# Rotary partners in a decoder layer: a TensorE matmul in place of partition-moving DMAs

## The reference, cut to what matters

```python
def rope_partial(t, cos, sin):            # t: (B, S, heads, 2, 64); only the first 16 of 64 dims turn
    half = ROT_DIM // 2                   # 8
    t1 = t[..., :half]
    t2 = t[..., half:ROT_DIM]
    rot = jnp.concatenate([t1 * c - t2 * s, t2 * c + t1 * s], axis=-1)
    return jnp.concatenate([rot, t[..., ROT_DIM:]], axis=-1)

# per head, two softmaxes over 64-dim halves, causal, in blocks of 128 queries:
p = softmax(mask(q_c k_c^T / 8));   a = p[0] - lam * p[1];   out = a @ v
```

## Time and profile before

| | |
|---|---|
| median of three executions | 1784.95 us |
| the profiled execution, its own time | 1784.95 us |
| its span, first to last instruction | 1783.2 us |
| PE busy | 1574.5 us (88%) |
| DVE busy | 1300.6 us (73%) |
| ACT busy | 546.8 us (31%) |
| POOL busy | 707.3 us (40%) |

### The profile page before, as it was taken

How to read it: one execution, slowest core, us unless ns; L and a number is a source line. 1 busy time by engine, 2 the same in 40 slices (tenths; PEclk the granted TensorE clock), 3 DMA queues, 4 the chain that set the end, 5 groups by cost and what they waited for, 6 DMA issues and landing times.

```text
span 1783.2 us, 20596 instructions
## 1 busy us (share of the span) xinstructions
PE 1574.5 (88%) x7020; PEld 1165.1 (65%) x7020; DVE 1300.6 (73%) x2421; ACT 546.8 (31%) x1337; POOL 707.3 (40%) x598
## 2 busy tenths in 40 slices
PE   3998999988997999999997999997999989999800
PEld 2787877776876999888886888885444434444300
DVE  5766456677455598999997789898566656666798
ACT  2442245534623642111113888884000000000001
POOL 1000111100001565633566566566644445444672
PEclk7999999999998999999998999999999999999955
DMA  8424421234421544999999999999999999999994
GB/s 325 164 95 151 159 74 57 78 109 163 169 95 48 179 157 181 408 367 357 367 383 363 327 363 369 339 358 334 387 409 409 409 412 409 409 409 409 409 401 188
DMA packets 126280, 499.18 MB, mean 280 GB/s; under 512 B 15456, under 2 KB 15840, under 8 KB 115808
## 3 DMA queue, kind: packets, MB, share of 16 engines
q0 software_dynamic: 75776, 269.52, 39.2%
q1 hardware_dynamic: 50400, 228.35, 33.6%
HBM read 492.04 MB, written 4.72 MB: 279 GB/s over the span
## 4 chain that ended last, share of the span: by engine, by line
DVE 34%; DMA 25%; PE 23%; ACT 6%; issue 4%; POOL 3%; DVEq 3%; ACTq 1%; SPq 0%
DMA ring<-in_up,idx 20%; DVE ring L1453 7%; DVE accum L1662 6%; PE bank L746 5%; PE bank L494 5%; PE bank L495 5%; PE bank L496 5%; DMA ring<-in_down,idx 4%; POOL ring L1687 3%; PE bank L733 2%; DVE acc_ada L1111 2%; DMA raw<-in_ada 1%; ACT whi L781 1%; DVE top_i L1490 1%; DVE top_i L1475 1%
## 5 line engine op out<-in xcount | busy, mean ns | idle before, releaser
L759 PE MATMUL bank<-stream,wmat 128*128 128x512 f32 x1024 | 443.7, 596 | 13.7 <-DMA stream<-in_up 7.0
L746 PE MATMUL bank<-h2T,stream 128*128 128x256 f32 x2048 | 451.6, 380 | 0.0
L1662 DVE SCALAR_TENSOR_TENSOR accum<-ring,share,accum 128x1024 f32<-128x1024 f32 x256 | 328.9, 1285 | 165.1 <-DMA ring<-in_up,idx 159.4
L1687 POOL DMA_INDIRECT ring<-in_down,idx x256 | 330.1, 1290 | 237.9 <-DVE pre L1453 184.5
L746 PEld LDWEIGHTS bank<-h2T,stream 128*128 128x128 f32 x2048 | 385.6, 190 | 50.6 <-issue 0.3
L759 PEld LDWEIGHTS bank<-stream,wmat 128*128 128x128 f32 x1024 | 195.9, 192 | 260.9 <-issue 246.2
L1687 POOL DMA_INDIRECT ring<-in_up,idx x256 | 263.8, 1030 | 233.1 <-DVE accum L1662 193.2
L1453 DVE CUSTOM_DVE_ANT_0 ring<-ring,h2row 128x1024 f32<-128x1024 f32 x256 | 306.0, 1220 | 42.0 <-DMA ring<-in_down,idx 38.6
L494 PE MATMUL bank<-hT_hi,whi 128*128 128x512 f32 (+1 forms) x640 | 232.1, 363 | 22.1 <-DVE hT_lo L1164 11.8
L495 PE MATMUL bank<-hT_lo,whi 128*128 128x512 f32 (+1 forms) x640 | 225.5, 352 | 0.0
L496 PE MATMUL bank<-hT_hi,wlo 128*128 128x512 f32 (+1 forms) x640 | 225.4, 352 | 0.0
(11 more groups left out here) (212 smaller groups left out, 1668.2 us busy)
## 6 DMA issues: line engine op xcount, KB each, us to landing
stream<-in_downT SPq DMA_DIRECT2D x128, 512.0 KB, 6.7
stream<-in_up SPq DMA_DIRECT2D x128, 512.0 KB, 6.8
raw<-in_ada SPq DMA_DIRECT2D x24, 1024.0 KB, 5.6
raw<-in_w_query SPq DMA_DIRECT2D x16, 1024.0 KB, 4.9
raw<-in_w_xp SPq DMA_DIRECT2D x4, 1024.0 KB, 6.0
raw<-in_w_gateA SPq DMA_DIRECT2D x4, 1024.0 KB, 4.8
raw<-in_w_branchP SPq DMA_DIRECT2D x4, 1024.0 KB, 4.8
raw<-in_w_q SPq DMA_DIRECT2D x4, 1024.0 KB, 4.7
```

Of the source, the lines that this page charges most:

```text
L746: last = pe.matmul(bank[:, 4 + i % 2, 0:DT], stream[:, i % RING, k * P:(k + 1) * P], h2T[:, k, GB * P:S], start=(k == 0), stop=(k == KT - 1))
L759: last = pe.matmul(bank[:, 2 * tb + half, :], wmat[:, i, tb * P:(tb + 1) * P], stream[:, (ET + i) % RING, half * S:(half + 1) * S], start= ...
L1662: dve.scalar_tensor_tensor(accum[:, b, :], ring[slot][:, :], share[:, b, k:k + 1], accum[:, b, :], ALU.mult, ALU.add).then_inc(sum_done, 1)
L1687: pool.indirect_dma_start(out=ring[slot][:, :], out_offset=None, in_=table, in_offset=bass.IndirectOffsetOnAxis(ap=idx[:, b, k:k + 1], axi ...
```

## The change

The partner exchange is done by PE. A constant 128x128 matrix `rotm` (128 more columns in the constants' transfer) holds -1 and +1 at the partners' places, and `rotate(n)` multiplies it with the `q_raw` tile into PSUM bank 6, the bank of the transposes. DVE reads the bank in place of `q_rot`. The sign moves out of the sine table into the matrix. The buffer `q_rot`, its zeroing and the 64 DMAs go. PE gets waits: a rotation waits for ACT's copy into `q_raw`, for the copy of all transposes issued so far and for the rope before; a `turn` waits until the ropes of all earlier slots have read the bank. The first rope of each group moves from slot 5 to slot 4.

```diff
-TURN_AT = {12 * (c - 1) + s: 4 * c + r for c in range(4) for r, s in enumerate((5, 7, 10, 13))}
+TURN_AT = {12 * (c - 1) + s: 4 * c + r for c in range(4) for r, s in enumerate((4, 7, 10, 13))}
...
+            def rotate(n):
+                c, r = n // 4, n % 4
+                wait_emptied(pe, "q" if r < 2 else "k", 2 * c + r % 2)
+                pe.wait_ge(trs_ready, sum(1 for g in UNIT_AT if g + TR_AFTER <= [s for s in TURN_AT if TURN_AT[s] == n][0]))
+                if n:
+                    pe.wait_ge(rot_used, n)
+                pe.matmul(bank[:, 6, :], rotm, q_raw[:, n % 2, :], start=True, stop=True)\
+                  .then_inc(rot_ready, 1)
...
             def turn(u):
...
+                pe.wait_ge(rot_used, sum(1 for s in TURN_AT if s < [g for g in UNIT_AT if UNIT_AT[g] == u][0] + TR_AFTER))
...
             def woven(g):          # PE; behind scores, turn and values of the slot
+                if g in TURN_AT:
+                    rotate(TURN_AT[g])
...
             def rope(n):           # DVE
-                dve.wait_ge(rot_in[n % 2], 64 * (n // 2 + 1))
+                dve.wait_ge(rot_ready, n + 1)
...
-                dve.tensor_tensor(q_tmp[:, 1, :], q_rot[:, n % 2, :], rope_sin[:, :], ALU.mult)
+                dve.tensor_tensor(q_tmp[:, 1, :], bank[:, 6, :], rope_sin[:, :], ALU.mult)
...
-            for n in range(16):    # POOL: partners(n) and its four DMAs each
-                partners(n)
...
                     # constants
+        if r < ROT // 2:
+            c[p + ROT // 2, C_ROT + p] = -1.0
+        elif r < ROT:
+            c[p - ROT // 2, C_ROT + p] = 1.0
-            c[p, C_FREQ] = inv[r % (ROT // 2)] * (-1.0 if r < ROT // 2 else 1.0)
+            c[p, C_FREQ] = inv[r % (ROT // 2)]
```

More of the change, by code:

```diff
@@ L49 @@
 PI_BELOW = 3.1415925
-C_ID, C_MASK, C_FREQ, C_INV, C_IOTA = 0, 128, 256, 257, 273
-C_W = 273 + 128
+C_ID, C_ROT, C_MASK, C_FREQ, C_INV, C_IOTA = 0, 128, 256, 384, 385, 401
+C_W = 401 + 128
 K_C, K_BADA, K_BGATE, K_PSCALE, K_GMIX, K_GFFN, K_SUBLN = 0, 8, 56, 72, 80, 88, 96
@@ L242, in layer @@
         ident = cst[:, C_ID:C_ID + P]
+        rotm = cst[:, C_ROT:C_ROT + P]
         mask = cst[:, C_MASK:C_MASK + P]
@@ L271, in layer @@
         q_tmp = place("q_tmp", [P, 2, S], f32, 144)
-        q_rot = place("q_rot", [P, 2, S], f32, 160)
         sigB = place("sigB", [P, KT, S], f32, 148)
@@ L367, in layer @@
         lam_exp = sem("lam_exp")
-        rot_in = [sem(f"rot_in{n}") for n in range(2)]
+        rot_ready = sem("rot_ready")
         rot_used = sem("rot_used")
@@ L859, in woven_tile @@
                 if stage == "gateB":
-                    if i == 6:
-                        act.wait_ge(rot_used, 16)
                     act.activation(sigB[:, i, :], tile(stage, i), ACT.Identity,
@@ L1702, in wlo_make @@
                 pool.sem_inc(qraw_free, 1)
[L1704 to L1717, removed]
-            for n in range(16):
-                partners(n)
-            for n in POOL_CHUNKS[1:]:
+            for n in POOL_CHUNKS:
                 wlo_make(n)
```

## The result

The changed kernel takes 1801.01 us (median of seven executions, 1798.86 to 1804.76); the kernel before, run beside it, takes 1784.34 us (seven, 1776.91 to 1787.41). The ratio is 1.0094, with a 95% interval from 1.0079 to 1.011: slower by 16.7 us. The profiled execution took 1803.89 us, its span is 1801.9 us. The forecast was 1800.5 us.

The account below looks back on a forecast made before the run. PE was taken as nearly full, busy 131.3 of 135.0 us, with DVE almost as late. Slot costs 2.6 + 0 + 9.0 + 2.5 + 0.5 + 1.0 = 15.6 us on 1784.95 gave 1800.5 us, range 1791 to near 1810.

Parts of the forecast that it names:

- The DMAs were hidden: Woven stage: only one of 16 ropes waited for partner DMAs, 5.9 us, so removing the 64 gives nothing by itself.
- A rotation costs 0.86 us of PE: Each of sixteen rotations holds PE 0.86 us, 13.8 us in all; its result is readable 1.02 us after its start.
- the case 1791 us: Rival: rotations overlap with projections, about 4 us of PE instead of 13.8, leaving 6 us slower; chance 0.05.
- DVE reads PSUM at no cost: Rope's sine multiply reading PSUM instead of SBUF: 0 us extra.
- Slots -8 to 1: First four rotations: 2.6 us in slots -8, -5, -2; 0 in slot 1, at most 1.0, given a 1.60 us wait.
- Slots 4, 16, 28: Moved ropes ahead of maxima: rotation 0.86 plus a new turn wait of 0.75, 1.6 us per slot.
- Slots 7, 10, 13 and 37: Slot 7 pays the plain rotation, 0.9 us; the others delay rope, maxima and the turn by 1.0 us each.
- Slot 34: Late rope makes the turn wait for its end, 1.9 us, less 1.43 us of PE idle time: 0.5 us.
- the clock as a rival: Form of the bank rival, 371 to 441 us: longer PE waits lower the clock, up to 3.5 us more; shared chance 0.14.
- Absorbing waits: Rival: PE's waits absorb rotations, +1.0 us, and three moved ropes give back 6.2 us: 1779.8 us; chance 0.10.
- A shared bank that decides in most slots: Rival: turns wait for rope ends in twelve other slots, up to 1 us each, 12 us more: 1812 us; chance 0.14.
- Freed POOL and DMAs: Rival: freeing POOL, DMA engines and the first rope's wait gains 5.9 us: 1779 us; chance 0.03.

Follow-up runs that it names:

- the doubled rotation: The changed kernel with each rotation issued twice into the same bank: 1812.71 us, ratio 1.0168 to the kernel before.
- constants alone: The kernel before with only the constants' transfer widened by 128 unused columns: 1782.25 us, ratio 0.9999.
- some maxima ahead: The changed kernel with DVE doing maxima ahead of the rope in slots 1 or 4 modulo 12: 1796.64 us, ratio 1.0073 to the kernel before.
- the move alone: The kernel before, DMAs kept, with the first rope of each group in slot 4 instead of 5: 1785.95 us, ratio 1.0020.
- the matmuls alone: The kernel before, DMAs and ropes kept, plus an unread f32 matmul of the rotation's size in each of sixteen rope slots: 1794.30 us, ratio 1.0064.
- first slot 5: The changed kernel with the first rope of each group back in slot 5: 1802.84 us, ratio 1.0113 to the kernel before.
- the version that beats both: The kernel before with maxima ahead of ropes, second conditioning chunk two slots later, its column sums one weight chunk later: 1775.39 us, ratio 0.9958.

## Why the prediction was right, step by step

**The DMAs were hidden: right.** The 64 transfers and POOL's work are gone (40.8 us of busy POOL), and no time came of it.

**A rotation costs 0.86 us of PE: right.** The chain of waits through slots 4 to 8 of the changed kernel:

```profile
259.63 0.88 PE bank L529 x2
260.53 0.69 DVE q_tmp L1313
...
263.18 1.23 DVE att_max L1287
...
266.76 0.76 DVE comb L1302
...
273.38 0.86 PE bank L529 x2
```

There are 32 records, two per matmul, and the rope's first multiply starts at 260.53, 1.07 us after 259.46; the forecast had 1.02. The gap of about 131 ns for 512 columns in the Trainium skill, page "TensorE: Matmul & The Clock Gate", section "Back-to-back issue gap", would have made the rotation 0.26 us and the case 1791 us. The trace and the doubled rotation (0.78 us each) speak against taking it here.

**DVE reads PSUM at no cost: right.** The sine multiply, ns min/median/max:

```profile
L1314 DVE TENSOR_TENSOR q_tmp<-bank,rope_sin x16: 682/683/684, 218.7 to 413.4; 128x512 f32<-128x512 f32 x16
```

From SBUF it took a median of 684 ns.

**Slots -8 to 1: right,** 2.7 for 2.6 us and 0.0 for 0. The wait ahead of unit 1's turn fell from 1.60 to 0.76 us: by the 0.84 of the rotation, which it took in.

**Slots 4, 16, 28: right in size and mechanism.** The chain above is the one forecast: rotation, rope, maxima, exponentials, `comb`, turn. The new waits of PE are 0.83, 0.84 and 0.82 us; 0.75 was forecast. They follow slots 4, 16 and 28 at the turn of slot 6, 18 and 30. From the forecast's eleven waits for `comb` and three new ones, ten are left: three of about 0.2 us (one of them at 272.38) are filled up, and the one at slot 35 ends with the rope instead.

**Slots 7, 10, 13 and 37: right,** 0.6, 1.1, 1.2 and 1.1 us for 0.9, 1.0, 1.0 and 1.0. Slot 7 costs less because PE's 0.2 us wait at its turn went; I had not subtracted it.

**Slot 34: the wait right, too small in size, because the clock was left out.** The forecast was 1.9 us for the rope's end less 1.43 us of idle time, 0.5. The turn waits for L1316, as said, and for 3.53 us. Its shift is 2.3 us more than that of the turn before it: 1.9, and 0.4 because DVE was by then 0.24 us later than PE and the handover took 0.15 us. What was missing is the clock. After the idle stretch PE did the slot's work at the lower level, 1.2 of 2.4 GHz. Granted clock is the third value from the end, first in the changed kernel:

```profile
398.50:405.30 6.80, 5.44 (x26) 5.47 (x27) 4.16 (x8) 2.10 (x6) 0.00 (x0) 0.50 0.34 140
```

and before, where the lower level ended ahead of the slot's end:

```profile
381.10:384.50 3.40, 3.40 (x19) 3.40 (x18) 2.65 (x5) 0.39 (x1) 0.00 (x0) 0.50 0.57 239
```

The other execution of the code of before (constants alone) had the clock full from the same turn, at 382.82, to the scores of unit 24, and PE stood for 2.92 us ahead of these scores in place of 1.43:

```profile
382.80:389.20 6.40, 3.46 (x29) 3.29 (x29) 4.42 (x9) 2.10 (x6) 0.00 (x0) 1.00 0.46 193
```

```profile
389.15 0.49 PE L545 MATMUL bank<-kT,qT 64*128 64x128 f32 x4 [2.92 <-ACT prob L823]
```

From that turn to the scores are 6.33 us in both executions, since ACT ends the wait. The scores start 2.31 us after ACT's exponentials of unit 23 in both. In the changed kernel they should have done the same:

```profile
384.11 0.69 ACT L823 ACTIVATE prob<-bank,att_bias 128x512 f32<-128x512 f32 x1 [8.12 <-DVE att_bias L1278]
```

```profile
401.82 0.69 ACT L836 ACTIVATE prob<-bank,att_bias 128x512 f32<-128x512 f32 x1 [8.36 <-DVE att_bias L1289]
```

The exponentials are 17.7 us later: 3.4 by the start of the stage, 14.1 by all slots before, and only 0.2 here. So the forecast was right that the probabilities are hardly delayed. The scores follow after 3.81 us and not 2.31: PE itself was late. Its work from the turn to the scores took 405.63 - 399.86 = 5.77 us, where it had 386.42 - 380.09 - 1.43 = 4.90 before and 6.33 - 2.92 = 3.41 at full clock. So of the 1.7 us at the scores (1.6 at the turn of unit 23) about 0.2 are the later ropes and 1.5 the low clock. That is the mis-sized term: 1.6 us in place of 0.5. The forecast named the clock as a rival and did not put it into this slot's sum, and the 1.43 us that it took off was itself what one stretch of low clock had left of the 2.92.

When the clock falls, no run here explains. One and the same code had 3.4 us at the lower level in one execution and none in the other, with a wait of 2.1 us at this turn in both. In the kernel with some maxima ahead PE waited as long as in the changed one, 3.54 us, and the clock stayed full:

```profile
396.00:400.00 4.00, 3.11 (x28) 2.94 (x27) 2.26 (x5) 2.10 (x6) 0.00 (x0) 1.00 0.07 27
```

What the change did here is to use up the slack. The turn moved 2.1 us closer to the end of ACT's work, which leaves about 0.9 of the 2.92 us (with some maxima ahead 0.89 were left). Before, a low stretch that cost PE 1.5 us (4.90 - 3.41) went into the wait; now one that costs 2.4 us (5.77 - 3.41) meets 0.9 us of slack, and 1.5 us get through. The profiles fit this: of the five kernels with the rotation, four have PE late at these scores, by 0.4 to 1.7 us, while before, the move alone, the matmuls alone and the constants alone have it on time. How often the clock is low there, one profile of each kernel cannot say.

**The sum.** 17.2 us in the stage for 15.6, and 16.7 us in the timed medians. Of the 1.6 us between them 1.1 are slot 34. The other slots make 15.6 us for 15.1, with small misses of both signs: slot 7 was forecast too dear, slots 4, 10 and 13 a little too cheap. The same from the engine's side: 13.8 us of rotations, plus PE's waits of the stage, which rose from 14.6 us (12.8, 1.4 and 0.4) to 17.1 (12.7, 3.5 and 0.9), make 16.3. The other 0.9 us fit the lower clock: against before it cost 5.77 - 4.90 = 0.9 us more ahead of the scores of unit 24, and from the turn of unit 25 to the scores of unit 28 are 6.86 us where 6.55 were.

**The rivals.** Absorbing waits: the rotation of slot 1 was absorbed, as forecast, but the total of the waits rose. The moved ropes paid nothing (0.4 us lost by the move alone). A shared bank that decides in most slots: a rope ended a wait once, at slot 35, and behind slot 4 the rope was done before the next turn came. The kernel with first slot 5 shows how it would look. The form with the clock did come, once, in slot 35: 1.5 of the up to 3.5 us that it was given. Cheap rotations: refuted by the doubled ones. Freed POOL and DMAs: nothing came of them.

## What to carry to other kernels

Before moving work to another engine to save transfers, look who waits for the transfers: here nobody did, and each of sixteen 0.86 us matmuls went to an engine that is busy for 131 of 135 us. If DVE must wait for a new producer, look at what stands behind the wait in its queue: putting the work that doesn't need it ahead gave back 4.7 of 17.2 us with three lines, and the same idea in the old kernel was part of the version that beats both. When a delayed step is spread out, list its consumers on other engines first; the one forgotten here took 5.5 us. And before a microsecond or two at one place is put down to a change, look at the same place in a second execution of the same code: here the clock alone differed there.

## What the runs showed of the hardware that was not expected

- The place where PE's clock drops moves between executions of the same code: in the slots around 35 the lower level covered 3.4 us in one execution of the code of before and none in the other; 6.8 us in the changed kernel and none with some maxima ahead. PE's work there took 3.41, 4.90 or 5.77 us. In the two executions of the code of before the difference went into a wait and cost nothing; in the changed kernel, whose slack there is smaller, 1.5 us of it got through.
- The stage of the same code repeated to 0.1 us between two profiled executions (227.97 and 228.06), although the start of the stage differed by 2.8 us and the rest of the span by 5.1 us.
- The rotation with f32 operands is two records, each in work for 0.60 us and holding PE for about 0.43 us; in fp32r it is one record of 0.46 us.
